# A two-block transformer kernel: in the second block's mixer, dense products dealt in rounds between the steps of the attention and delta-rule chains

## What is computed

```
def hybrid_mixer(x, w_in, conv_w, a_log, dt_bias, dn_norm_g, sink, w_branch_a, w_branch_b, w_out, pos_bias):
    hcat = x @ w_in                                   # 1024 x 7696: the dense products
    qa, ka, va, qkv_b, beta_raw, dt_raw, z, gate_raw = split(hcat)
    ya = sliding_window_attention(qa, ka, va, pos_bias, sink) @ w_branch_a      # 16 heads, 4 kv heads
    qkv_b = silu(causal_depthwise_conv_2(qkv_b, conv_w))                        # 4 taps, 3072 channels
    qb, kb, vb = l2norm(q), l2norm(k), v
    o = gated_delta_rule(qb, kb, vb, g, beta)                                   # 8 heads
    o = rms(o) * dn_norm_g * silu(z)
    yb = o @ w_branch_b
    return (sigmoid(gate_a) * ya + sigmoid(gate_b) * yb) @ w_out
```

## Time and profile before

| what | us |
|---|---|
| median of 3 runs | 3669.57 (3665.37 to 3671.03) |
| profiled execution, span of the core's instructions | 3663.0 |
| TensorE matmuls busy | 3199.0 (87%) |
| VectorE, ScalarE, GpSimd busy | 2032.9, 1313.3, 902.9 |
| mixer chains of layer 0 in the second block, 1896.5 to 2365.4 | 468.9 |

### The profile page before, as it was taken

The page is one execution under the profiler, slowest core; times in us unless marked ns, Lnnn a source line. Parts: engine busy times, 40 slices in busy tenths (PEclk is TensorE's granted clock), DMA queues, the critical chain, the costliest instruction groups (busy, mean ns, idle before and its releaser), DMA issues.

```text
span 3663.0 us, 57483 instructions
## 1 busy us (share of the span) xinstructions
PE 3199.0 (87%) x22178; PEld 2990.0 (82%) x22178; DVE 2032.9 (55%) x3046; ACT 1313.3 (36%) x1898; POOL 902.9 (25%) x425
## 2 busy tenths in 40 slices
PE   7998798989998799988977778889899778778897
PEld 7988798989988798988966777789889677767897
DVE  4558766545568566554543544475555435454754
ACT  3343344333343334332333322333333333233332
POOL 0034572000054462000042333230100423332301
PEclk9998999999998899999977888899999778889899
DMA  5543344554543245556522211145455221211453
GB/s 194 185 166 104 105 152 163 185 176 157 184 165 101 96 146 174 184 170 203 197 93 70 70 58 63 62 158 188 167 184 196 92 71 69 70 58 64 160 185 126
DMA packets 72104, 495.34 MB, mean 135 GB/s; under 512 B 8000, under 2 KB 8176, under 8 KB 19856
## 3 DMA queue, kind: packets, MB, share of 16 engines
q1 hardware_dynamic: 67504, 471.95, 37.8%
q0 software_dynamic: 4048, 18.59, 2.0%
q10 hardware_dynamic: 272, 0.99, 0.1%
HBM read 487.31 MB, written 4.19 MB: 134 GB/s over the span
## 4 chain that ended last, share of the span: by engine, by line
issue 67%; POOL 17%; PE 7%; DVE 4%; DVEq 1%; ACT 1%; POOLq 1%; DMA 1%; ACTq 0%; SPq 0%
POOL weights_low L851 15%; PE psum L947 6%; POOL small L811 1%; DMA weight_ring<-stream 1%; PE psum L950 1%; DVEq L2145 1%; DVE small L1938 1%; DVE normed_t_low L1759 1%; ACT weights_high L1433 0%; DVE normed_t_high L1757 0%; POOLq L810 0%; POOL work L899 0%; POOLq L873 0%; POOL residual L874 0%; DVE work L2051 0%
## 5 line engine op out<-in xcount | busy, mean ns | idle before, releaser
L947 PE MATMUL psum<-normed_t_high,weights_high 128*128 128x256 f32 x4832 | 1410.1, 292 | 36.3 <-DVE normed_t_low L1759 32.5
L947 PE MATMUL psum<-normed_t_low,weights_high 128*128 128x256 f32 x4832 | 1390.9, 288 | 0.0
L947 PE MATMUL psum<-normed_t_high,weights_low 128*128 128x256 f32 x4832 | 1389.1, 287 | 0.0
L1433 ACT ACTIVATE weights_high<-weight_ring 128x2048 fp32r<-128x2048 f32 (+1 forms) x464 | 859.3, 1856 | 1461.6 <-DMA weight_ring<-stream 1453.9
L1750 DVE TENSOR_TENSOR weights_low<-weight_ring,weights_high 128x2048 fp32r<-128x2048 f32 x292 | 672.3, 2306 | 697.3 <-ACT weights_high L1433 694.8
L947 PEld LDWEIGHTS psum<-normed_t_high,weights_high 128*128 128x128 f32 x4832 | 953.2, 197 | 49.7 <-DVE normed_t_low L1759 37.0
L947 PEld LDWEIGHTS psum<-normed_t_low,weights_high 128*128 128x128 f32 x4832 | 953.1, 197 | 4.5
L947 PEld LDWEIGHTS psum<-normed_t_high,weights_low 128*128 128x128 f32 x4832 | 951.0, 197 | 0.0
L851 POOL TENSOR_TENSOR weights_low<-weight_ring,weights_high 128x2048 fp32r<-128x2048 f32 (+1 forms) x172 | 725.1, 4219 | 875.0 <-ACT weights_high L1433 875.0
L947 PE MATMUL psum<-weights_high,work_parts 128*128 128x512 f32 x1664 | 524.3, 396 | 13.2 <-DVE work_parts L1759 13.2
L947 PE MATMUL psum<-work 128*128 128x128 f32 (+3 forms) x2000 | 358.6, 330 | 113.7 <-DVE work L2199 45.4
(11 more groups left out here) (187 smaller groups left out, 2489.0 us busy)
## 6 DMA issues: line engine op xcount, KB each, us to landing
weight_ring<-stream SPq DMA_DIRECT2D x400, 1024.0 KB, 4.8
weight_ring<-stream SPq DMA_DIRECT2D x64, 768.0 KB, 4.2
feature_rows<-feat POOLq DMA_DIRECT2D x6, 1024.0 KB, 4.9
work<-toeplitz_rows POOLq DMA_DIRECT2D x8, 512.0 KB, 7.1
feature_rows<-feat POOLq DMA_DIRECT2D x6, 512.0 KB, 4.0
toeplitz_rows<-work POOLq DMA_DIRECT2D x1, 3072.0 KB, 36.0
params<-prms POOLq DMA_DIRECT2D x5, 251.5 KB, 3.1
residual<-x SPq DMA_DIRECT2D x1, 1024.0 KB, 7.5
```

What stands on the lines that cost most here:

```text
L947: return pe.matmul(dst, lhsT, rhs, start=start, stop=stop, skip_group_check=True)
L1433: return act.activation(dst, src, ACT.Copy, scale=scale)
```

## The change

The dense units of the second block's mixer are cut into rounds. `interleave` replaces `weave`: after every chain step it gives out the next share of the rounds, `total * (n + 1) // len(chain)` of them by step n. A unit's first shares are `part` steps (only TensorE does something in them), and its last share is the unit's own step (the host), whose `first` says how many rounds are done. In the attention the first half now has two q units and the three convolution units of the first delta group (80 rounds over 24 steps), the second half the four z units (64 rounds over 24). A delta group has the next group's three convolution units and then its two gates (80 rounds over 46 steps); the last group has two gates (32 rounds). The splits can be made in quarters of a unit (`quarters`, `some`), and `close` has a rule for parts and another for the rest. The stream's order, and so the layout of the weights, follows the plan. The first block's plan keeps its order. Helper functions `mm` and `transpose` are written out, which changes line numbers alone.

```diff
+QUARTERS = 4
...
-        self.low = []
+        self.by = []
         for i, key in enumerate(self.stream):
             after_ffn = any(k[0] in ("gu", "d") for k in self.stream[max(0, i - 3):i])
-            by = "pool" if key[0] in self.by_pool and not after_ffn else "vector"
-            self.low.append((by, self.tick("low_by_" + by, 1)))
-            self.tick("high_ready", 1)
+            self.by.append("pool" if key[0] in self.by_pool and not after_ffn else "vector")
+            self.tick("low_by_" + self.by[-1], QUARTERS)
+            self.tick("high_ready", QUARTERS)
             self.tick("slots_free", 1)
             self.tick(("slot", i % SLOTS), 16)
-
-
-        used, split, short = 0, 0, True
+        self.low_at = [QUARTERS * sum(b == by for b in self.by[:i + 1]) for i, by in enumerate(self.by)]
+
+        used, high, low, short = 0, 0, 0, True
         for n, st in enumerate(self.steps):
-            used += st.unit is not None
-            if st.unit is not None:
-                short = any(x.kind in ("post", "post2") for x in self.steps[n + 1:n + 3])
-            upto = min(used + AHEAD - short, self.units) if used or st.kind in ("norm", "xt") else 0
-            while split < upto:
-                st.split.append(split)
-                split += 1
-        assert split == self.units
+            if st.kind == "part":
+                used += st.a == 0
+                at = QUARTERS * (used + 1) + QUARTERS * st.a // st.src.rounds
+                to_high, to_low = at + 1, at
+            else:
+                if st.unit is not None:
+                    used += st.first == 0
+                    short = any(x.kind in ("post", "post2") for x in self.steps[n + 1:n + 3])
+                ahead = 1 if st.first else AHEAD - short
+                to_high = QUARTERS * (used + ahead) if used or st.kind in ("norm", "xt") else 0
+                to_low = to_high
+            last = QUARTERS * self.units
+            if min(to_high, last) > high:
+                st.high, high = quarters(high, min(to_high, last)), min(to_high, last)
+            if min(to_low, last) > low:
+                st.low, low = quarters(low, min(to_low, last)), min(to_low, last)
+        assert high == low == QUARTERS * self.units
+
+
+def quarters(a, b):
+
+    out = []
+    while a < b:
+        n = min(b, (a // QUARTERS + 1) * QUARTERS)
+        out.append((a // QUARTERS, a % QUARTERS, n - a))
+        a = n
+    return out
...
+def interleave(pl, chain, dense):
+
+
+    total = sum(rounds for rounds, _ in dense)
+    given, done, later = 0, 0, []
+    todo, host = list(dense), None
+    for n, f in enumerate(chain):
+        f()
+        if later:
+            later.pop(0)()
+        upto = total * (n + 1) // len(chain)
+        while given < upto:
+            if host is None:
+                rounds, make = todo.pop(0)
+                host, rest = make()
+                done = 0
+            give = min(upto - given, host.rounds - done)
+            if done + give < host.rounds:
+                pl.steps.append(Step("part", None, src=host, a=done, b=done + give))
+            else:
+                host.first = done
+                pl.steps.append(host)
+                later += rest
+            given, done = given + give, done + give
+            if done == host.rounds:
+                host = None
+    assert host is None and not todo
...
-    dense = [project_q[2:4] + project_z[0:2], project_z[2:4] + [lambda w=w: conv(0, w) for w in range(3)]]
+    dense = [[(16, lambda p=p: query(p)) for p in (2, 3)] + [(16, lambda w=w: conv(0, w)) for w in range(3)],
+             [(16, lambda p=p: gated(p)) for p in range(4)]]
...
-        weave(pl, chain, evenly(chain, dense[half]))
+        interleave(pl, chain, dense[half])
...
-        convs = [lambda w=w, hp=hp: conv(hp + 1, w) for w in range(3)] if hp + 1 < NH_B // 2 else []
-        dense = {1: gates[2 * hp:2 * hp + 1], 3: gates[2 * hp + 1:2 * hp + 2]}
-        dense.update({pos: [g] for pos, g in zip((15, 23, 31), convs)})
-        weave(pl, chain, dense)
-    gates[8]()
-    gates[9]()
+        dense = [(16, lambda w=w, hp=hp: conv(hp + 1, w)) for w in range(3)] if hp + 1 < NH_B // 2 else []
+        dense += [(16, lambda k=k: gate(0, k)) for k in range(2 * hp, 2 * hp + 2)]
+        interleave(pl, chain, dense)
...
+        def some(tile, i, q, n):
+            w = width(i) // QUARTERS
+            return tile[:, i % SLOTS, q * w:(q + n) * w]
...
-                    pool.wait_ge(high_ready, reach("high_ready", i + 1))
-                    raw, high = RING[:, i % SLOTS, 0:width(i)], HIGH[:, i % SLOTS, 0:width(i)]
-                    pool.tensor_tensor(LOW[:, i % SLOTS, 0:width(i)], raw, high.bitcast(F32), ALU.subtract
-                                       ).then_inc(low_by_pool, 1)
+                    pool.wait_ge(high_ready, reach("high_ready", QUARTERS * i + q + n))
+                    pool.tensor_tensor(some(LOW, i, q, n), some(RING, i, q, n), some(HIGH, i, q, n).bitcast(F32),
+                                       ALU.subtract).then_inc(low_by_pool, n)
...
+            def product(st, a, b, fresh=None):
+
+                job = st.jobs[0]
+                w = weights(st, KB, a == 0)
+                if a == 0:
+                    pe.wait_ge(bank_taken[job.bank], turn_at(job))
+                for r in range(a, b):
+                    c, k = r // KB, r % KB
+                    if fresh is not None and c == 0 and k % 2 == 0:
+                        ready = named(("xt", fresh)).jobs[k // 2]
+                        pe.wait_ge(bank_taken[ready.bank], taken_at(ready))
+                    for m, (i, j) in enumerate(PARTS):
+                        ins = pe.matmul(PS[:, job.bank, c * S:(c + 1) * S], w[i][:, k, c * P:(c + 1) * P], XT[j][:, k, :],
+                                        start=(k, m) == (0, 0), stop=(k, m) == (KB - 1, 2), skip_group_check=True)
+                        if (r, m) == (0, 0):
+                            pay(ins)
+                if b == st.rounds:
+                    ins.then_inc(bank_full[job.bank], 1)
+                    owed[0] += 1
+
...
+            def part(st):
+                host = st.src
+                if host.kind == "gy":
+                    gate_product(host, st.a, st.b)
+                elif host.kind in ("pv",) or host.what in ("cv", "dv"):
+                    product_by_tokens(host, st.a, st.b)
...
-            def split_high(i):
+            def split_high(i, q, n):
 
                 act.wait_ge(slot_loaded[i % SLOTS], loaded_at(i))
-                copy(HIGH[:, i % SLOTS, 0:width(i)], RING[:, i % SLOTS, 0:width(i)]).then_inc(high_ready, 1)
+                copy(some(HIGH, i, q, n), some(RING, i, q, n)).then_inc(high_ready, n)
```

More of the change, by code:

```diff
@@ L140, in step @@
             self.stream.append(unit)
-        self.steps.append(st)
         if name is not None:
             self.named[name] = st
+        return st
+    def step(self, kind, name=None, banks=(), signals=(), unit=None, **args):
+        st = self.make(kind, name, banks, signals, unit, **args)
+        self.steps.append(st)
         return st
@@ L381, in plan_second @@
             signals=[("small_proj_ready", 1), ("small_logs_ready", 1), ("log_decay_ready", 1)])
-    project_q = [lambda p=p: pl.step("pq", ("pq", p), banks=["lo"], p=p, unit=("w", p)) for p in range(4)]
-    project_q[0]()
-    project_q[1]()
+    for p in range(2):
+        pl.steps.append(query(p)[0])
     pl.step("pv", "pv", banks=["lo"], unit=("w", 5))
@@ L1044, in pb @@
             def pb(st):
+                product(st, st.first, st.rounds, fresh=1 if st.p == 0 and st.kind == "pb" else None)
+            def product(st, a, b, fresh=None):
                 job = st.jobs[0]
[L1046 to L1049 removed]
```

275 lines of the change are left out of this document (143 added, 132 removed).

## The result

The changed kernel takes 3686.85 us (median of 4 runs, 3678.29 to 3688.62), the kernel before 3669.11 us (4 runs, 3665.37 to 3671.03). The ratio is 1.0042, with a 95% interval from 1.0028 to 1.0056: slower by 0.4%. The forecast was 3641 us, 0.8% faster; its range, 3580 to 3695, holds the time, its sign is wrong.

The account below looks back on a forecast made before the run. The prediction took engine-to-engine latency in the chains, plus TensorE's half clock after idling, as the bound. Per layer, -23 attention, +7.5 delta groups and +1 group 3 made -14.5; two layers, -29, gave 3641 us, range 3580 to 3695.

Parts of the forecast that it names:

- hold: Some 7.4 us from a unit's first matmul (5.5 transfer, 1.9 split) when ScalarE takes nothing that stands behind the split.
- just fits under: Attention: a turn stands about 7 us behind its own score, and 7.4 us of ScalarE waiting was said to fit there.
- the clock rises to 0.88 in half 1: Attention half 1: TensorE's mean clock taken as 0.88, adding 5.4 us to 47.3 at full clock.
- the small terms for clock and waits: Delta groups 0 to 2: 1.5 us for `du4` to `dot`; clock 0.87 adds 8.5 us, a third swallowed by idle pieces.
- a sum without any term for the clock: Group 3: 29 + 11.3 + 7.5 + 5.7 + 4 = 57.5, say 58 us against 56.9, 1 us lost.
- It is nearly free now: Kernel before, delta groups: 48 dense matmuls and two `dla` steps cover ScalarE's wait; the `dlb` behind waits 0.48 us.
- Attention, 67 and 53 us: Attention halves 0 and 1 forecast at 67 and 53 us, against 78.4 and 65.1: 23 us a layer saved.
- Delta groups, 92 us: Groups 0 to 2: 86.8 us at full clock, 92 with the clock, against 92.1, 88.7 and 87.7; 7.5 us a layer lost.
- Rival 3: Slower: uncovered waits in delta groups, each followed by a cold clock restart; 25 us a layer lost, 3720 us, chance 0.13.
- rivals 2 and 3: The first is balance: attention gains 3 us less, a group loses 4 more, 3665 to 3675 us, chance 0.12.
- Rival 1: Much faster: filling hides the waits, ScalarE's lag saves them; 3573 us if half goes, 3513 if all, chance 0.19.
- That the change doesn't do what it says: Whole mixer: quarter splits do not exist in the order, so whole ones stay; called half true already, and counted on.

Follow-up runs that it names:

- e7: The kernel before, dense units still woven whole, with the second block's mixer weights asked for two units ahead in place of three: 3594.3 us, ratio 0.9786.
- e1: The changed kernel with whole splits made two units ahead, not three, while units are dealt out: 3542.9 us, ratio 0.965.
- e2: The changed kernel with chain steps between a unit's parts asking for no splits, so splits come in quarters: 3475.8 us, ratio 0.9467.
- e6: e2 with ScalarE's high part of a unit made whole, GpSimd's low part still in quarters: 3502.9 us, ratio 0.954.
- e5: e2 with GpSimd's low part of a unit made whole, ScalarE's high part still in quarters: 3529.5 us, ratio 0.9608.

## Why the prediction went wrong

Three steps failed, in order of their weight: in the attention that a hold "just fits under" the time between score and turn, and that the clock rises to 0.88 in half 1; in the delta groups the small terms for clock and waits, and in group 3 a sum without any term for the clock; and, in the account of before, "It is nearly free now". The details follow.

**What bounds the kernel: right, with one sentence wrong.** The chains are bound by latency and the clock after idling, and the hold is real, 7.4 us long and whole. But the step "It is nearly free now" failed. It rested on one `dlb` that waited 0.48 us, one place among a layer's 26 units. e7 puts the price of the holds before, with the low parts that go with them, at 76 us. The sentence enters no term of the sum, which sets measured stretches of before against estimates of after; what it hid was the larger change that was to be had. One way in which they cost stands in the trace of before, and was overlooked. The split is followed by GpSimd's low part, and VectorE's small operations stand while it runs. GpSimd, VectorE and TensorE of the kernel before, in half 0:

```profile
1917.40 4.50 POOL L851 TENSOR_TENSOR weights_low<-weight_ring,weights_high 128x2048 fp32r<-128x2048 f32 x1 [14.88 <-ACT weights_high L1433]
```

```profile
1918.80 3.14 DVE L1938 TENSOR_SCALAR small<-small 128x2 f32<-128x2 f32 x1
```

```profile
1921.99 0.92 PE L947 MATMUL psum<-work 64*128 64x128 f32 x4 [2.86 <-DVE small L1938]
```

Two numbers per partition take 3.14 us, and TensorE idles for 2.86. Of the eight such operations in half 0, three take 2.2 to 3.1 us, all beside a low part, and the other five 0.23; in e7 this one takes 0.23 too. By these rows I estimate that for such a step the hold is up to 11.9 us (7.4 and 4.5), not 7.4.

**Attention, 67 and 53 us: the terms that failed most.** Half 0 took 70.8 and 69.9 us, half 1 60.3 and 59.3: 20.3 us too little forecast in the two layers, 13.6 of them in half 1. There the step was "a hold of 7.4 us just fits under it", where "it" was set at about 7 us, already less than the hold. It didn't fit: the waits behind the holds (1.96 us of TensorE at 1990.85, 1.82 and 2.69) sum to 6.5 where 3.3 was set, and the clock stayed at 0.81 where 0.88 was set "since the idle pieces are fewer". For 39.5 us of work at full clock the forecast allowed 44.9 busy us; it took 50.3. So in half 1 of layer 0 the clock was 5.4 us of the error and the idle time 2.2. ScalarE's and TensorE's rows at the first of the three waits:

```profile
1988.50 1.91 ACT L1500 ACTIVATE weights_high<-weight_ring 128x2048 fp32r<-128x2048 f32 x1 [1.88 <-DMA weight_ring<-stream]
1990.32 0.47 ACT L1500 ACTIVATE work<-psum 128x384 f32<-128x384 f32 x1
```

```profile
1990.85 0.90 PE L1210 MATMUL psum<-constants,work 128*128 128x128 f32 x3 [1.96 <-ACT work L1500]
```

Short as this idle piece is, TensorE comes out of it at the half clock, so fewer long pieces didn't mean a faster clock:

```profile
1987.00:1988.90 1.90, 1.88 (x12) 1.29 (x10) 0.68 (x5) 0.40 (x1) 0.00 (x0) 1.00 0.40 164
...
1990.85:1992.50 1.65, 1.65 (x8) 1.65 (x9) 0.00 (x0) 1.50 (x6) 1.65 (x1) 0.50 0.00 0
```

**Delta groups, 92 us: right in mechanism, 0.7 to 3 us short.** They took 94.4, 92.7 and 94.1, and 94.3, 95.0 and 93.0. In group 1 the piece ahead of `ddc` was 7.3 us (plus 0.8 ahead of `dtf`) for the 10.0 predicted, though `dtr` to `dtf` took the 16 us forecast. The four holds left 3.05 (1.29 ahead of a `dla`, put down to VectorE, and 1.76 ahead of the `dlb`), 3.81, 4.16 and 5.12 us for 3.6, 4.1, 5.0 and 5.4. The remaining terms, clock and small waits, were set too low: 66.5 busy us for 57.2 of work, where 57.2 and two thirds of 8.5 were summed. Over six groups that is 11.5 us. Group 3 took 60.5 and 60.2 for 58, another 4.7. Its sum had no term for the clock at all, and gave no reason; granted were 0.86 and 0.85, and TensorE was busy for 45.4 us in layer 0 for the 40.3 of work that were summed.

**The sum.** The forecast doubled layer 0, but layer 1 was 6.0 us shorter before, so the same 454 us would have saved 6.0 less in it. 20.3 + 11.5 + 4.7 + 6.0 = 42.5 us turn the 30 that the stretches were to save (469.0 less 454, twice) into the 12.5 they cost. The gates behind them and small drifts make it 13.6 in the span. The median stands 10.2 us above the span in place of 6.6; neither number is what lies around the span, which is 1.7 us in the profiled execution, and the rest of the 10.2 is that this execution was the fastest of the four. So no single term has the wrong sign. The forecast was a difference of two large amounts, -46 in the attention and +17 in the groups; the one came out as -25.1 and the other as +37.6.

**The clock.** In these two stretches of layer 0 it mostly fell as the idle time (length less busy time) grew:

| stretch | idle us, granted clock |
|---|---|
| half 1 | before 11.9, 0.81; change 10.0, 0.81; e7 8.0, 0.84; e1 6.1, 0.90; e2 3.5, 0.89 |
| group 1 | change 26.2, 0.85; before 18.3, 0.87; e1 16.2, 0.91; e7 15.7, 0.92; e2 10.6, 0.95 |

But the idle time alone doesn't fix it. e7's six full groups idle for 15.4 to 16.5 us each and were granted 0.86 to 0.92, and e2's half 1, with the least idle time of the table, has a lower clock than its group 1. For half 1 the forecast set 7.8 us of idle time and 0.88, where e7 has 8.0 and 0.84. For a group it set 29.6 us (10.0, 18.1, 1.5) and kept the 0.87 that went with 18.3. The rule weighed in the prediction, from the Trainium skill, "TensorE: Matmul & The Clock Gate", section "HAM oscillation — how this bites in real kernels", pointed the right way, and the trace agrees with it at 2207.51 (0.41 us a matmul, behind 5.12 us of idle time). The same shows behind the 1.96 us at 1990.85.

**The rivals.** Rival 3's mechanism was at work, but at half its price or less. Attention saved 12.4 us in layer 0, close to the 13 it said, but by luck: it had the clock stay at 0.76 in half 0, where it rose to 0.87, and half 1 fell short instead. A group lost 4 us in layer 0 and 6 in layer 1, in place of 11. Its turning point of 97 us was worked out with 23 us saved in the attention; with 12.4 it is at about 93. The outcome lies between rivals 2 and 3. Rival 1 did not come about: the holds are all there, as was argued against it. But its two prices, 3573 and 3513 us (the second is 3519 by the terms that it gives), come within 40 us of what the same dealing gives once the holds are gone: 3543 (e1) and 3476 (e2).

**That the change doesn't do what it says: right, and the main point.** The page counts 464 rounding instructions before and in the changed kernel, 614 in e2. e2 shows what the change would have brought had its quarter splits existed: -5.3%. The cause is one line. A chain step between two parts still asks for everything up to three units ahead, so the rest of the unit is taken at once.

## What to carry to other kernels

When a transfer's wait stands in an in-order engine's queue, ask for it as late as its user allows, and look at everything behind it in that queue before dealing other work into the gap: here that was worth 2.1% without the dealing and 3.9% with it. Cut pieces of background work that share an engine with a latency-bound chain down to the length of a chain step. And where a forecast is the difference of a gain and a loss, work out how far each may be off together: here 46 and 17 us stood for a net of 29, both came out 21 us worse, and the sign was given 0.75 to 0.13.

## What the runs showed of the hardware

**VectorE stands while GpSimd runs a low part.** The grouped rows of the same operation, `silu`, in the kernel before, the changed kernel, e1 and e2 (one fence each; busy us and mean ns behind the bar):

```profile
L2128 DVE SCALAR_TENSOR_TENSOR work<-work 128x512 f32<-128x512 f32 x24 | 32.4, 1349 | 1.9 <-ACT work L1652 1.9
```

```profile
L2194 DVE SCALAR_TENSOR_TENSOR work<-work 128x512 f32<-128x512 f32 x24 | 97.2, 4050 | 39.9 <-ACT work L1719 39.9
```

```profile
L2197 DVE SCALAR_TENSOR_TENSOR work<-work 128x512 f32<-128x512 f32 x24 | 46.7, 1948 | 8.7 <-ACT work L1722 8.7
```

```profile
L2198 DVE SCALAR_TENSOR_TENSOR work<-work 128x512 f32<-128x512 f32 x24 | 16.5, 689 | 8.7 <-ACT work L1723 8.7
```

One instruction, six times as long by what GpSimd does beside it. In the changed kernel 22 of the 24 begin inside a low part and take 4355 ns on average; the other two, and those outside a low part in the other kernels, take 691 to 693 on average. In e2 none begins inside one. `taps`, which reads one operand from PSUM and one from SBUF, is the control: 481 to 482 ns in all four, though in the kernel before 86 of its 144 begin inside a low part (in the changed kernel none does). The Trainium skill, "SBUF — State Buffer", section "Who interferes with whom", says that a VectorE instruction with two SBUF inputs, or in a two-port mode such as `tensor_scalar` can enter, contends with a GpSimd instruction that reads SBUF, and that the later one fully blocks. The rows agree: at 2151.96 in the changed kernel `silu` took 4.57 us beside a low part of 4.53 that had begun at 2151.46. In the changed kernel's group 1 no idle piece of TensorE over 1.3 us names VectorE as its releaser, so there this lay mostly behind the holds. In e1 two small multiplications in front of `dl0` took 3.67 us so, and TensorE idled for 2.68; in e2 that piece is down to 0.81.

**Smaller pieces cost the background engines little.** ScalarE's roundings take 884 us in 614 pieces (e2) for 859 in 464 (e1), GpSimd's low parts 752 us in 308 for 726 in 172: 25 us more on each, for 67 us less in all. The Trainium skill, "Perfetto Trace Analysis", section "Optimizing Scalar/DVE Operations", says that breaking up instructions may let work finish sooner where these engines cause bubbles without being full. e6 against e2 shows it for ScalarE (27 us); e5 against e2 shows the like for GpSimd (54 us), of which that section doesn't speak.
